# Prompt attention in blocks of 256 queries instead of 128, with the window mask added in PSUM

## What is computed

```
# C: blocks of 128 queries; each sees its own and the previous 128 keys
s = einsum('bnqkgd,bnskd->bnkgqs', qb, kb) * (hd ** -0.5)        # hd 64, 4 query heads
s = where(kpos <= qpos and kpos > qpos - 128 and kpos >= 0, s, -inf)
p = softmax(concatenate([s, sink]))[..., :-1]
o = einsum('bnkgqs,bnskd->bnqkgd', p, vb)
# D: the same keys for every query, 256 memory tokens, 4 heads
s = einsum('blhd,bmhd->bhlm', q, mk) * (hd ** -0.5)
p = softmax(s)
o = einsum('bhlm,bmhd->blhd', p, mv)
# both, in the group's output
c_out = o.reshape(B, L, 256) * silu(z)
```

## Time and profile before

| | |
|---|---|
| median of three runs | 2365.94 us |
| the profiled execution's own time | 2365.44 us |
| its span, first to last instruction | 2363.6 us |
| TensorE matmuls (PE) busy | 2325.7 us, 98% |
| VectorE (DVE) busy | 1369.8 us, 58% |
| ScalarE (ACT) busy | 918.0 us, 39% |
| share of TensorE in the chain that ended last | 95% |
| granted TensorE clock | 0.999 |

### The profile page before, as it was taken

One profiled execution on the slowest core, in us unless ns is written; L12 is line 12 of the kernel. 1 busy time (PEld: TensorE's weight loads), 2 busy tenths in 40 slices (PEclk: granted clock), 3 DMA queues, 4 the chain that ended last, 5 costly groups with the idle time before them and its releaser, 6 DMA issues.

```text
span 2363.6 us, 40015 instructions
## 1 busy us (share of the span) xinstructions
PE 2325.7 (98%) x14532; PEld 1845.8 (78%) x14532; DVE 1369.8 (58%) x3346; ACT 918.0 (39%) x2111; POOL 108.2 (5%) x179
## 2 busy tenths in 40 slices
PE   8999999999999999999999999999999999999998
PEld 4677777787788888878877777777878888787877
DVE  4566746565456765655536767365644676555443
ACT  4444324344434333344434543153434443233331
POOL 1000000001000000000000000000100000000000
PEclk9999999999999999999999999999999999999999
DMA  7110212244210122223331111132340113142132
GB/s 242 28 54 21 62 36 63 58 157 131 71 46 20 42 65 75 67 65 125 135 90 36 28 45 46 50 94 92 131 122 20 53 29 74 25 108 60 47 117 80
DMA packets 230557, 172.12 MB, mean 73 GB/s; under 512 B 56886, under 2 KB 206908, under 8 KB 230332
## 3 DMA queue, kind: packets, MB, share of 16 engines
q1 hardware_dynamic: 226100, 154.78, 22.8%
q10 hardware_dynamic: 4264, 14.78, 1.8%
HBM read 136.60 MB, written 21.93 MB: 67 GB/s over the span
## 4 chain that ended last, share of the span: by engine, by line
PE 95%; DVE 2%; issue 1%; ACT 1%; DMA 1%; ACTq 0%; SPq 0%; DVEq 0%; POOL 0%; POOLq 0%
PE bank L1725 53%; PE bank L2749 16%; PE bank L1820 3%; PE bank L2020 3%; PE bank L1978 3%; PE bank L1965 2%; PE bank L1804 2%; PE bank L1168 1%; PE bank L1797 1%; PE bank L1866 1%; PE bank L1962 1%; PE bank L2765 1%; PE bank L1860 1%; PE bank L1772 1%; PE bank L2010 1%
## 5 line engine op out<-in xcount | busy, mean ns | idle before, releaser
L1725 PE MATMUL bank<-h_hi,w_hi 128*128 128x512 f32 (+3 forms) x2160 | 484.5, 361 | 11.3 <-DVEq L2290 4.1
L1725 PE MATMUL bank<-h_lo,w_hi 128*128 128x512 f32 (+3 forms) x2160 | 488.7, 363 | 1.8
L1725 PE MATMUL bank<-h_hi,w_lo 128*128 128x512 f32 (+2 forms) x2080 | 468.2, 362 | 1.5
L1725 PEld LDWEIGHTS bank<-h_hi,w_hi 128*128 128x128 f32 (+1 forms) x2160 | 354.0, 186 | 89.4 <-issue 31.6
L1725 PEld LDWEIGHTS bank<-h_lo,w_hi 128*128 128x128 f32 (+1 forms) x2160 | 351.1, 185 | 73.6 <-issue 15.4
L1725 PEld LDWEIGHTS bank<-h_hi,w_lo 128*128 128x128 f32 x2080 | 343.5, 188 | 69.0 <-issue 16.2
L2749 PE MATMUL bank<-scr_r,tb_r 128*128 128x512 f32 x816 | 195.1, 395 | 2.1 <-ACT scr_r L2089 1.6
L2749 PEld LDWEIGHTS bank<-scr_r,tb_r 128*128 128x128 f32 x816 | 151.7, 188 | 36.8 <-issue 3.4
L2070 ACT ACTIVATE tb<-bank 128x512 f32<-128x512 f32 (+1 forms) x140 | 71.2, 508 | 192.8 <-PE bank L1725 186.6
L2229 ACT ACTIVATE scr<-bank 128x512 f32<-128x512 f32 x132 | 77.9, 590 | 170.3 <-PE bank L1978 169.0
L2428 DVE COPY_PREDICATED scr<-level_mask,bank 128x128 f32<-128x128 uint8 (+1 forms) x332 | 116.7, 351 | 45.6 <-PE bank L1820 26.9
(11 more groups left out here) (289 smaller groups left out, 3117.3 us busy)
## 6 DMA issues: line engine op xcount, KB each, us to landing
w_raw<-in_w_in SPq DMA_DIRECT2D x96, 512.0 KB, 3.7
out<-scr SPq DMA_DIRECT2D x32, 512.0 KB, 2.7
scr<-in_w_out SPq DMA_DIRECT2D x16, 512.0 KB, 4.9
w_raw<-in_w_out SPq DMA_DIRECT2D x16, 512.0 KB, 3.5
scr<-in_x_prompt SPq DMA_DIRECT2D x16, 512.0 KB, 3.7
scr<-out SPq DMA_DIRECT2D x16, 512.0 KB, 3.3
rot<-out ACTq DMA_DIRECT2D x12, 512.0 KB, 3.7
mix_t<-in_x_prompt ACTq DMA_DIRECT2D x8, 512.0 KB, 13.8
```

Source lines behind the costliest of these rows:

```text
L1725: m = mm(bank[b][0:m_w, 0:c1 - c0], w[:, slot, k, 0:m_w], h[:, k, c0:c1], start=it["piece"] == 0 and k == 0, stop=it["piece"] == 2 and k = ...
```

## The change

Scores, softmax, transposes and values of a prompt step are done for two blocks of 128 queries at a time: a step has 2 pairs in place of 4 blocks. Sample steps keep their form. Banks 6 and 7 are now filled fully (two blocks of 256 columns each), a `turn` fills banks 2 and 3, the value of pair c goes to bank 4 + c with 256 columns. There is one buffer of probabilities and one of transposed probabilities, each twice as large, so the exponentials of pair 1 wait for the transposes of pair 0, and the copy of the transposes of pair 1 for the values of pair 0. For C the mask is added in place in PSUM, and the exponentials read PSUM, so banks 6 and 7 stay taken until ScalarE has read them, as for D before.

```diff
-ATT_P = layout([("p0", ST), ("p1", ST), ("pt0", ST), ("pt1", ST)])
+PAIRS = ST // CH // 2
+ATT_P = layout([("p", 2 * ST), ("pt", 2 * ST)])
...
+            for c in range(PAIRS) if not sample else ():
+                out.append(item("score", [6, 7], step=s, c=c))
+            for c in range(PAIRS) if not sample else ():
+                out.append(item("turn", [2, 3], step=s, c=c))
+                out.append(item("value", [4 + c], step=s, c=c, j=0))
...
+    def behind_turn(soft):
+
+        if soft["kind"] != "soft" or soft["step"]["st"] == "s" or soft["c"] == 0:
+            return False
+        return ("turn", soft["step"]["n"], soft["c"] - 1) not in placed
...
                         for h in range(2):
                             hp = slice(HD * h, HD * h + HD)
-                            ql = q[hp, CH * c:CH * c + CH]
                             emptied(pe, it, 6 + h)
...
+                            for i in range(2):
+                                blk = 2 * c + i
+                                ql = q[hp, CH * blk:CH * blk + CH]
+                                dst = bank[6 + h][:, 256 * i:256 * i + 256]
+                                if unit == "C":
+                                    k = key_copy(s)[hp]
+                                    pr = k_prev[hp, g, :] if blk == 0 else k[:, CH * (blk - 1):CH * blk]
+                                    mm(dst[:, 0:CH], ql, pr, start=True, stop=True)
+                                    m = mm(dst[:, CH:2 * CH], ql, k[:, CH * blk:CH * blk + CH], start=True, stop=True)
+                                else:
+                                    m = mm(dst, ql, mem_kt[hp, g, :], start=True, stop=True)
                             m.then_inc(bank_full[6 + h], 1)
...
+                            for h in range(2):
+                                for i in range(2):
+                                    o = 2 * 256 * h + 256 * (b - 2) + P * i
+                                    m = nc.tensor.transpose(bank[b][:, (2 * h + i) * P:(2 * h + i + 1) * P], p[:, o:o + P], ident[:])
...
                     for h in range(2):
                         out = bank[b][HD * h:HD * h + HD]
...
+                            for j in range(2):
+                                for i in range(2):
...
+                                    o = 4 * P * j + (2 * h + i) * P
+                                    m = mm(out[:, CH * j:CH * j + CH], v, pt[:, o:o + P], start=i == 0, stop=i == 1)
...
+                    if not sample and it["c"] > 0:
+
+                        turn_read(act, s, it["c"] - 1)
...
+                        for x in range(4):
+                            h, i = x // 2, x % 2
+                            m = fn(p[:, 256 * x:256 * x + 256], bank[6 + h][:, 256 * i:256 * i + 256], ACT.Exp, bias=z[:, 4 + x:5 + x],
+                                   scale=1.0 if unit == "C" else HD ** -0.5, accum_out=z[:, 12 + x:13 + x])
                         m.then_inc(exp_done, 1)
...
+                        act.drain().then_inc(bank_free[6], 1)
+                        act.drain().then_inc(bank_free[7], 1)
...
-                        fn(pt, bank[b][:, 0:n], ACT.Copy).then_inc(bank_free[b], 1)
+                        fn(pt.rearrange("p (b n) -> p b n", b=2), psum[:, 2:4, :], ACT.Copy).then_inc(bank_free[2], 1)
+                        act.drain().then_inc(bank_free[3], 1)
...
+                            at = [psum[:, 6:8, 256 * i:256 * i + 256] for i in range(2)]
...
+                                link(stt(at[i], at[i], scale, mask.to_broadcast([P, 2, 256]), ALU.mult, ALU.add))
...
+                            link(nc.vector.tensor_reduce(top, psum[:, 6:8, :].rearrange("p h (i n) -> p h i n", i=2), X, ALU.max))
```

More of the change, by code:

```diff
@@ L137, with keeps_banks @@
 TABLE_US = 1.28
+def keeps_banks(soft):
+    return soft["step"]["unit"] == "D" or soft["step"]["st"] != "s"
 def banks_of(it):
@@ L394, in last_reader @@
         return None
-    end = ST // CH - 1 if u["st"] != "s" else 0
+    end = 0 if u["st"] == "s" else ST // CH - 1 if u["unit"] == "B" else PAIRS - 1
     if row == 3:
@@ L555, in plan_units @@
     held_by, rest_until = {}, [0.0]
+    n_scores = [0]
     turning = [len(group) * (2 if group[0]["unit"] == "C" else 0) for group in groups]
@@ L564, in emit @@
         kind, n, c = it["kind"], it["step"]["n"] if "step" in it else 0, it.get("c", 0)
-        while any(x["kind"] == "soft" and x["step"]["unit"] == "D" and set(x["of"]["bank_list"]) & set(banks_of(it))
+        while any(x["kind"] == "soft" and keeps_banks(x) and set(x["of"]["bank_list"]) & set(banks_of(it))
                   for _, _, x in parts):
@@ L568, in emit @@
         if kind == "score":
-            while sum(x["kind"] in ("soft", "scale") for _, _, x in parts) >= STATS - 1:
+            it["no"] = n_scores[0]
+            n_scores[0] += 1
+            while any(x["kind"] in ("soft", "scale") and x["of"]["no"] <= it["no"] - STATS for _, _, x in parts):
                 emit_part("soft", "scale")
@@ L572, in emit @@
             while ("scale", n, c) not in placed:
-                emit_part("soft", "scale")
+                emit(parts.pop(next(i for i, x in enumerate(parts) if x[2]["kind"] in ("soft", "scale") and not behind_turn(x[2])))[2])
         elif kind == "fac_prod":
@@ L631, in emit_parts @@
             for when, eng, it in parts:
-                if it["kind"] not in kinds and when <= max(fc.t["PE"], fc.t[eng]):
+                if it["kind"] not in kinds and not behind_turn(it) and when <= max(fc.t["PE"], fc.t[eng]):
                     emit_part(it["kind"])
@@ L707, in ready @@
         part = {"turn": ("scale", n, c), "fac_prod": ("fac_exp", n, it.get("i", 0)), "gla_norm": ("spread", n, 0)}.get(kind)
-        held = [when + PART_US["held"] for when, _, x in parts if x["kind"] == "soft" and x["step"]["unit"] == "D"
+        held = [float("inf") if behind_turn(x) else when + PART_US["held"] for when, _, x in parts if x["kind"] == "soft" and keeps_banks(x)
                 and set(x["of"]["bank_list"]) & set(banks_of(it))]
@@ L1392, in units @@
         swa_steps = [it["step"]["n"] for it in items if it["kind"] == "rope_k"]
+        exps = [(it["step"]["n"], it["c"]) for it in items if it["kind"] == "soft"]
+        scales = [(it["step"]["n"], it["c"]) for it in items if it["kind"] == "scale"]
         sample_att = [it["step"]["n"] for it in items if it["kind"] == "cache_t"]
@@ L2541, in on_vector @@
                     lay = lay_of(s)
-                    p = area(lay, "p" + par(it))
+                    p = probs_of(s, "p")
                     z = stat[:, it["seq"] % STATS]
                     scale = HD ** -0.5
-                    nh = 1 if sample else 2
-                    if not sample and c >= 2:
-                        tb_, tu = next(iter(att_uses[("turn", s["n"], c - 2)].items()))
-                        dve.wait_ge(bank_full[tb_], tu + 1)
-                    for h in range(nh):
-                        filled(dve, it, 6 + h)
+                    for b in it["banks"]:
+                        filled(dve, it, b)
                     if unit == "C":
```

181 lines of the change are left out of this document (83 added, 98 removed).

## The result

The changed kernel takes 2399.37 us (median of 4, 2398.21 to 2401.39), the kernel before 2366.37 us beside it on the same chip. The ratio is 1.0137, 95% interval 1.0122 to 1.0152. The forecast was 2340 us (2320 to 2370): it is 59 us short and has the wrong sign.

What follows compares the result with a forecast made beforehand. TensorE, busy 2325.7 of 2363.6 us, was taken as the bound. 2365.4 - 40.9 (less TensorE work) + 14.4 (waits) = 2338.9 us profiled; with the runs' median 0.5 above, forecast 2340 us (rounded up), range 2320 to 2370.

Steps and rivals of the forecast that it cites:

- The items: TensorE's scores and values, doubled in size and halved in number, would take 23.6 us less.
- the second half costs both heads 0.43 us together: Doubled scores and values: score of D becomes 1.06 us, score of C 1.08, value 1.02, if heads still overlap.
- rival 1: Score of C and value: heads no longer run beside each other; 2381 us, or 2422 if in series; chance 0.12.
- Changes of kind: TensorE switching between half-array and whole-array work: fewer switches, 17.3 us less.
- No wait in the first passes: First passes, without a sample step: projections and values cover the softmax chain, so no TensorE wait is expected.
- rival 2: The 30 attention steps outside the second place each lack 1 us of cover: 30 us more, 2370; chance 0.10.
- The second place: Unit C, g 1, st 1 of each second pass: TensorE idle 8.9 us against 1.7, adding 14.4 us in all.
- the 5.7: At the second place, TensorE idle 5.7 us of the 12.0 from pair 0's transposes to the values' end.

Runs made afterwards that it cites:

- Two and two: Changed kernel issuing two matmuls of head 0, two of head 1, repeated, in scores of C and values: 2358.51 us, ratio 0.9962.
- in turn: Changed kernel, heads alternating matmul by matmul in scores of C and values, pending scalings emitted before the sample's score: 2341.86 us, ratio 0.9898.
- scalings first: Pending scalings emitted ahead of the sample step's score: 2340.44 us on the two-and-two kernel, 2386.55 us on the changed kernel alone.
- the filled ones: Useless identity matmuls in TensorE's waits at the second place: two-and-two kernel 2358.27 us overlong, 2347.05 us shortened; heads alternating with scalings first 2342.55 and 2334.44 us.

## Why the prediction was wrong, step by step

- **The items (failed).** The step that failed is "the second half costs both heads 0.43 us together". It holds if the heads still run beside each other, and I gave that 0.66. With four matmuls of head 0 ahead of head 1's first they don't for half of the item: rival 1, which had 0.12 and was priced near the truth in its first form ("if it must wait for two of the four matmuls, each item costs 0.43 more", 2381). Measured: a score of C 1.64, a value 1.51, so 0.56 and 0.49 more than predicted. Two and two takes 0.45 and 0.44 of it away, 40.9 us off the kernel, and in turn takes nearly all of it. (The sum of the items is 23.7 and not 23.6; that changes nothing.)
- **The items, once overlapped.** With two and two, D's score was right (1.065), C's score (1.19 for 1.08) and the value (1.075 for 1.02) were too dear: 32 x 0.11 + 64 x 0.055 = 7 us. In turn, they have the predicted prices to 0.01 us. The earlier trace rows could not show it, since with two matmuls of each head the two orders differ by 0.007 us.
- **Changes of kind (held).** With two and two the first passes take 427.6 us instead of 437.6 and 437.5, the 10 us each that were predicted. The items give 8 x 0.20 + 8 x 0.11 + 16 x 0.11 = 4.2 of it, so some 5.7 is left for the changes of kind and the small waits, against 17.3 / 4 = 4.3.
- **No wait in the first passes (held).** The order of 20 projections and the values covers the chain; rival 2 did not come.
- **The second place (held in its waits, failed in its price).** 8.5 us idle for 8.9 predicted, at the instructions named (L2015, L1977, L1994, the projection). The single waits were off by more: the transposes 3.0 and the values 1.2, together less than the 5.7, and the projection at 0.7 was not named. But idle time was priced at its own length. What it also costs is TensorE's clock: 11.3 us for the two-and-two form.

The sum closes. From the forecast of 2340: 41 us for the lost overlap, 11 for the half clock, 7 for the items two and two against in turn give 2399, and 2399.4 was measured. The 11 is measured on the two-and-two kernel and taken over: no run filled the waits of the changed one, whose trace has 46 us at the lower level where the other has 42. Three small things are in none of these. TensorE's wait for `scr_r` in the output stage (L2782) rose from 1.6 to 4.9 us, and a score of D (L1997) waits 0.9 us in each second pass, both unforeseen; the changes of kind gave about 5 us more than predicted. They cancel, and that the sum closes to 1 us is in part luck.

I was wrong on rival 1 more by its chance than by its price (0.43 us for an item, against 0.56 and 0.49). The evidence against it was that two matmuls are passed now. That showed that there is a look-ahead and nothing of how deep it is, while the change doubled just that depth. And the rule in the Trainium skill (TensorE: Matmul & The Clock Gate, The mechanism), that matmuls start strictly in program order, is not what the rows show, neither for two nor for four: at 280.46 head 1's first record starts while three of head 0 are still to come. By the prediction's working four and four would have taken 2422 under that rule; the measurement, 2399, lies between that and the forecast. Setting it aside as refuted by the earlier trace rows was right in the letter and took away the warning that it held.

## What to carry to other kernels

When two groups of matmuls share the array and run beside each other by its halves, issue them in turn, one of each: the order costs nothing, two and two costs 0.05 to 0.1 us for an item of eight matmuls, four and four 0.49 to 0.55. Before items are made longer, ask for each overlap how many instructions one side must be passed by, and whether a row shows a run that long. And a wait of TensorE is not priced at its own length: where several of them stand together, look at the granted clock behind them, and fill the waits, or move what causes them, before anything else.

## What the runs showed of the hardware that I had not expected

- A matmul on the other half of the array starts ahead of matmuls issued before it, but in these traces only when no more than three of their records have not started (seen with runs of four, six and eight records of a head). Scores of C by the run length of a head: in turn 1.09, two 1.19, three 1.42, four 1.64 us; values 1.025, 1.075, 1.29, 1.51.
- Idle times of 1.8, 0.7, 1.1, 3.0, 1.2 and 1.3 us within 27 us, none of them long, went with a granted clock of 0.80 over 34 us of the two-and-two kernel, with TensorE busy for 24.8 of them. With the idle times filled it was 1.00. The Trainium skill (Perfetto Trace Analysis, Matmul Optimizations) says that the matmul engine scales its power with its utilization, and that matmuls should therefore be executed back to back. The trace agrees: here this is worth 11.3 of 2358 us, and useless matmuls in the waits are a way to get it.
- Whether half clock comes behind a given wait changes from run to run. With scalings first, where the waits left are of 1 to 2 us, the runs spread over 10 us (2338.7 to 2348.3 two and two, 2336.9 to 2346.6 in turn), the filled ones over 1 to 3. Why a drop comes in one run and not in the next stays open.
